# POOL issues both halves of one quad of cache pages, ahead of its operand pads; SP issues neither

## What is computed

```python
def layer(x, p, caches):
    q, kc, ks, kw, gates, u = split(rmsnorm(x, g_attn) @ w_in)       # ONE input projection
    # compressed branch: every block of 32 tokens (stride 16) of K and V goes through a small MLP
    past_cmp = cache_cmp[page_table].reshape(DB, past_len, 2, KVH, DH)  # 8 sequences x 32 pages
    cmp = compress(concat([past_cmp, kc]), w1, w2, pe)
    attn = gates . (attend(q, cmp), attend(q, selected_blocks(ks)), attend(q, window(kw)))
    conv = swish(layernorm(causal_depthwise_conv(u, width=31)))
    x = x + concat([attn, conv]) @ w_out
    x = x + relu(rmsnorm(x, g_mlp) @ w_up)**2 @ w_down
    x = x + (p @ w_ple) * sigmoid(rmsnorm(x, g_ple) @ w_ple_gate)
    return rmsnorm(x, g_final)

def compress(kv, w1, w2, pe):
    c = chunks_of_16_rows(kv)
    pre = c[:-1] @ w1[:, :16] + c[1:] @ w1[:, 16:] + pe_term
    return gelu(pre) @ w2
```

## Time and profile before

| what | value |
|---|---|
| time, median of 3 runs | 1845.31 us (1843.94 to 1849.23) |
| the profiled execution's own time | 1846.45 us |
| its span, first to last instruction | 1844.8 us |
| TensorE clock granted over the span | 0.993 of full |
| DMA | 198.31 MB, mean 107 GB/s |

### The profile page before, as it was taken

How to read it: one execution, slowest core, us unless ns; L and a number is a source line. 1 busy time by engine, 2 the same in 40 slices (tenths; PEclk the granted TensorE clock), 3 DMA queues, 4 the chain that set the end, 5 groups by cost and what they waited for, 6 DMA issues and landing times.

```text
span 1844.8 us, 36000 instructions
## 1 busy us (share of the span) xinstructions
PE 1792.5 (97%) x13796; PEld 1672.8 (91%) x13796; DVE 1058.4 (57%) x1802; ACT 720.5 (39%) x1355; POOL 747.9 (41%) x702
## 2 busy tenths in 40 slices
PE   8999999999999999999998999999989999999998
PEld 7999999999986667676997999999989999999998
DVE  6799965684657677767547844555631212224525
ACT  5312333335336576666424333333421212114435
POOL 2204972233304343444544665656522323225531
PEclk9999999999999999999999999999999999999999
DMA  4321366355313444342414222322531414113114
GB/s 155 129 69 47 112 205 155 97 134 142 107 62 110 144 125 123 116 133 76 140 46 146 97 103 105 116 102 97 188 129 50 137 45 142 41 48 96 58 35 140
DMA packets 178793, 198.31 MB, mean 107 GB/s; under 512 B 22580, under 2 KB 152304, under 8 KB 178103
## 3 DMA queue, kind: packets, MB, share of 16 engines
q1 hardware_dynamic: 168173, 172.67, 30.1%
q0 software_dynamic: 7840, 21.25, 4.1%
q10 hardware_dynamic: 2610, 2.10, 0.4%
HBM read 165.00 MB, written 35.55 MB: 109 GB/s over the span
## 4 chain that ended last, share of the span: by engine, by line
PE 57%; DVE 6%; ACT 2%; issue 2%; POOL 2%; DMA 1%; SPq 0%; ACTq 0%; DVEq 0%; POOLq 0%
PE ps L198 13%; PE ps L2644 11%; PE ps L204 6%; PE ps L2649 6%; PE ps L2416 5%; PE ps L1825 3%; PE ps L1813 3%; PE ps L1837 3%; PE ps L3252 2%; POOL S L1780 2%; PE ps L1864 2%; DVE S L2074 1%; PE ps L3262 1%; PE ps L3278 1%; PE ps L1900 1%
## 5 line engine op out<-in xcount | busy, mean ns | idle before, releaser
L184 POOL TENSOR_TENSOR wd_lo<-wd_raw,wd_hi 128x1024 fp32r<-128x1024 f32 (+1 forms) x40 | 100.5, 2513 | 256.2 <-ACT wd_hi L2961 256.2
L1780 POOL TENSOR_SCALAR S<-S,inv,gate_p 128x640 f32<-128x640 f32 (+7 forms) x186 | 124.9, 689 | 193.2 <-DVE inv L2084 193.2
L3065 DVE TENSOR_TENSOR xT<-ps,xT 128x1056 f32<-128x1056 f32 x40 | 50.3, 1258 | 257.2 <-PE ps L204 257.2
L198 PE MATMUL ps<-Hhi,wd_hi 128*128 128x352 f32 x768 | 167.7, 327 | 5.8 <-ACT wd_hi L2961 5.8
L198 PE MATMUL ps<-Hlo,wd_hi 128*128 128x352 f32 x768 | 166.8, 325 | 0.0
L1164 DVE SCALAR_TENSOR_TENSOR y<-u,conv_w,y 128x1024 f32<-128x1024 f32 x120 | 156.5, 1351 | 1.2
L1008 PE MATMUL ps_p<-Xhi,w1hi 128*128 128x256 f32 x544 | 139.1, 293 | 1.4 <-ACT Xhi L713 1.4
L431 POOL DMA_DIRECT2D raw<-in_cache_cmp_kv_dram x124 | 78.2, 634 | 149.3 <-DVE relaid L1250 120.8
L198 PEld LDWEIGHTS ps<-Hhi,wd_hi 128*128 128x128 f32 x768 | 132.1, 191 | 6.2 <-ACT wd_hi L2961 6.1
L1008 PE MATMUL ps_p<-Xlo,w1hi 128*128 128x256 f32 x544 | 132.7, 283 | 0.0
L198 PEld LDWEIGHTS ps<-Hlo,wd_hi 128*128 128x128 f32 x768 | 132.0, 190 | 0.0
(11 more groups left out here) (475 smaller groups left out, 4502.1 us busy)
## 6 DMA issues: line engine op xcount, KB each, us to landing
s_raw<-in_cache_slc_kv_dram SPq DMA_DIRECT2D x256, 128.0 KB, 2.1
raw<-in_cache_cmp_kv_dram SPq DMA_DIRECT2D x132, 128.0 KB, 4.3
hidden<-cs SPq DMA_DIRECT2D x32, 528.0 KB, 2.6
Hraw<-hidden SPq DMA_DIRECT2D x32, 528.0 KB, 4.9
up_raw<-in_w_up_dram SPq DMA_DIRECT2D x16, 1024.0 KB, 5.4
raw<-in_cache_cmp_kv_dram POOLq DMA_DIRECT2D x124, 128.0 KB, 4.6
win_raw<-in_w_in_dram SPq DMA_DIRECT2D x38, 256.0 KB, 3.4
wd_raw<-in_w_down_dram SPq DMA_DIRECT2D x16, 512.0 KB, 4.1
```

Of the source, the lines that this page charges most:

```text
L184: self.c.nc.gpsimd.tensor_tensor(self.lo[s][:, 0:nk, :], self.raw[s % self.raw_slots][:, 0:nk, :], self.hi[s][:, 0:nk, :].bitcast(F32), AL ...
L198: nc.tensor.matmul(ps[:, j, 0:CH], self.hi[s][:, k, :], x(k)[:, CH * j:CH * j + CH], start=(k == 0 and n == 0), stop=False)
L1780: nc.gpsimd.tensor_scalar(x, x, inv[:, n % 3, 3 * e + br:3 * e + br + 1], c.gate_p[:, i, H * br + h:H * br + h + 1], ALU.mult, ALU.mult).t ...
```

## The change

POOL's loop over its halves of quads gets a second loop behind it, still ahead of the wait for the projection's end: half 0 and half 1 of quad 4, eight transfers. Its later loop begins with quad 5 instead of 4. SP's list loses half 0 of quad 4. The two halves now count their landings on POOL's semaphore of slot 0, and `relay` asks for the counts that follow from that. Nothing else is changed; each engine computes what it did, and the same pages are read.

```diff
--- before.py
+++ after.py
@@ -428,7 +428,7 @@
                 pages = [cs_pages[ds(page, 1)] for page in at]
             for n, page in enumerate(pages):
                 half, i = n % 2, 2 * part + n // 2
-                eng.dma_start(raw[s][DH * half:DH * half + DH, i, :], page.rearrange("o q f -> (o q) f")).then_inc(raw_loaded[0 if g < 2 else part][s], 16)
+                eng.dma_start(raw[s][DH * half:DH * half + DH, i, :], page.rearrange("o q f -> (o q) f")).then_inc(raw_loaded[0 if g < 2 else 1 if g == 4 else part][s], 16)
 
         @block.sync
         def _(sp):
@@ -496,7 +496,7 @@
                     load_quad(sp, mybir.EngineType.SP, part, g)
             store_rows(8)
             spill_q(3)
-            for g in (2, 3, 4):
+            for g in (2, 3):
                 load_quad(sp, mybir.EngineType.SP, 0, g)
             sp.wait_ge(free[0], 10)
             for e in range(3):
@@ -591,11 +591,13 @@
             pool.wait_ge(pages_loaded, 16)
             for g in (2, 3):
                 load_quad(pool, mybir.EngineType.Pool, 1, g)
+            for part in range(2):
+                load_quad(pool, mybir.EngineType.Pool, part, 4)
             pool.wait_ge(W.done, NT)
             for s in range(2):
                 nc.gpsimd.memset(Xhi[s][:, :, 128:NC + 2].bitcast(F32), 0.0).then_inc(padded, 1)
                 nc.gpsimd.memset(Xlo[s][:, :, 128:NC + 2].bitcast(F32), 0.0).then_inc(padded, 1)
-            for g in range(4, 1 + NQD * B):
+            for g in range(5, 1 + NQD * B):
                 load_quad(pool, mybir.EngineType.Pool, 1, g)
 
             f = dict(allow_small_or_imprecise_dtypes=True)
@@ -1236,7 +1238,8 @@
             def relay(g):
                 s = g % 4
                 for part in range(2):
-                    after(dve, raw_loaded[part][s], 64 * (g // 4 + 1) + (64 - 128 * part if s < 2 else 0))
+                    by_pool = (128 * part - 64) if s == 0 and g >= 4 else 0
+                    after(dve, raw_loaded[part][s], 64 * (g // 4 + 1) + (64 - 128 * part if s < 2 else 0) + by_pool)
                 if g == 0:
                     dve.wait_ge(alo_read, 1)
                 elif g == 2:
```

## The result

| what | before | after |
|---|---|---|
| median time, 21 runs each | 1845.82 us (1841.5 to 1849.87) | 1850.84 us (1848.94 to 1856.77) |
| ratio of times | | 1.0025, 95% interval 1.0018 to 1.0032 |
| the profiled execution's own time, and its span | 1846.45, 1844.8 us | 1850.22, 1848.7 us |
| granted clock over the span | 0.993 | 0.99 |

The ratio is + 4.6 us, with an interval of + 3.3 to + 5.9 (the two medians lie 5.0 us apart): the way that was forecast, inside the 0.3% that the prediction called the same, on its slow side. The time lies inside the range (1843 to 1851.5 us), near the upper end, 3.6 us above the 1847.2 us of the forecast itself.

A forecast was written before the change was run, and what follows sets the result against it. PE, busy 97% of the span, was taken to bound the kernel. Pads + 3.94, quad 4's wait - 2.59, its clock - 1.48, clock after the longer hole + 2.0 sum to + 1.87: from 1845.31 to 1847.2 us, range 1843 to 1851.5.

The forecast's parts named there:

- The pads: POOL's memsets behind quad 4's issues: all come 3.94 us later, and PE's first hole grows from 1.40 to 5.34 us.
- rival 3: POOL's quad 4 issues: DVE's copies hold them up, pads 5.0 us later yet, + 6.9 us, 1852.2 us; chance 0.06.
- The wait for quad 4: DVE's relay 4: the data are there over 5 us ahead, so all 2.59 us of PE's second hole go.
- The clock: PE behind its holes: 1.48 us saved with the second hole, 2.0 us (0 to 2.83) lost behind the longer first.
- SP, the later halves, the transfers: SP's lighter list, POOL's halves from quad 5 on, and the same bytes moved: each counted as nothing.
- The sum: Whole kernel: + 3.94 - 2.59 - 1.48 + 2.0 = + 1.87 us, with the clock's ends - 0.13 to + 2.70 us.
- The range: Measured time, held at 0.8: 1843 to 1851.5 us, from the clock's ends, 2 us either way, part of two rivals.
- Rivals 1 and 2: 1: pads cost nothing, the hole goes, 1841.2 us, chance 0.10; 2: quad 4 is still late, 1851.3 us, chance 0.05.
- Rival 4: The change doesn't do what it says; pads slip further only if quad 0's relay is late; held by the rest, 0.03.

The follow-up runs named there:

- half of it: Kernel before, but POOL issues its own half of quad 4 ahead of the pads, SP keeps the other half: 1846.42 us, ratio 0.9997.
- pads by DVE (in either): DVE instead of POOL sets the four pads, in the kernel after (1845.40 us, ratio 0.9990) and in the kernel before (1844.61 us, 0.9989).
- 4 and 11 products: Kernel before with 4 or 11 chained scratch products on POOL ahead of the pads: 1846.48 us, ratio 0.9994, and 1848.40 us, 1.0014.
- pads first: Kernel after, but with the four pads ahead of quad 4's eight issues on POOL: 1847.24 us, ratio 0.9996.
- SP's quads first: Kernel before, but SP issues its halves of quads 2 to 4 ahead of storing the sampled rows: 1844.18 us, ratio 0.9984.
- pages early: Kernel after, with POOL's two readings of quad 4's page numbers put ahead of its wait for quad 2: 1845.06 us, ratio 0.9996.

## Why the prediction was right, and where it was short

One account fits every profile, to within 0.35 us, from the projection's end to the first copy of a compressed K. In the "half of it" run PE works from the first hole to that copy for 15.65 us without a stop at full clock; its own row therefore fits by construction. Add a run's holes, and half of what PE did at the lower clock (PE's busy time in that stretch):

| kernel | first hole | later hole | work at 0.50 | sum | measured |
|---|---|---|---|---|---|
| before, three profiles | 1.40 each | 2.59, 3.79, 2.91 | 3.41, 5.46, 3.41 | 21.35, 23.57, 21.67 | 21.12, 23.24, 21.46 |
| after, three profiles | 6.53, 6.40, 6.61 | none | 4.88, 3.04, 6.03 | 24.62, 23.57, 25.28 | 24.41, 23.41, 24.99 |
| pads by DVE (in either) | 1.58 | 1.66 | none | 18.89 | 19.15, 19.14 |
| half of it | 2.63 | none | none | 18.28 | 18.28 |
| 4 and 11 products | 3.18; 6.52 | none | 3.41; 5.51 | 20.54; 24.93 | 20.37; 24.65 |
| pads first | 1.40 | 2.28 | 3.42 | 21.04 | 20.91 |
| SP's quads first | 1.40 | none | none | 17.05 | 17.06 |
| pages early | 3.39 | none | 3.42 | 20.75 | 20.63 |

*The pads: right in kind, 1.2 us short.* The forecast had the first memset 3.94 us later. From the projection's end it came after 0.06 us before and 5.17, 5.06 and 5.26 after, so 5.1 later. Of the missing 1.2, 0.86 is the idle of 2.24 for 1.38 and 0.30 the idle of 0.36 inside the first half, 0.06 elsewhere. The cause of the 0.30 is not found. The step that failed stands in rival 3: "So at most the first issue meets one". It counted issues and left out the reading of page numbers ahead of the first, which is what ran beside DVE's split and relay 1, and the forecast gave even that one issue no price; its pace of 3.64 us for a half quad was read at 272 us, where relay 4 was still waiting. The Trainium skill (SBUF — State Buffer, two separate sides) has the rule for issues, and the 1.70 us issue agrees; quad 3's four issues in 2.27 us beside relay 0 show no such hold-up, and the slow reading of page numbers stands in our rows alone.

*The wait for quad 4: right, and somewhat larger.* It goes whole, and the landing was early by far: the last of quad 4 was there at 271.85, and its relay began at about 280. Over three profiles of before PE's second hole is 3.1 us, not the 2.59 of one.

*The clock: right by luck of a mean.* Half of the work at 0.50 is on average 2.0 us before (1.7, 2.7, 1.7) and 2.3 after (2.4, 1.5, 3.0). I had - 1.48 and + 2.0; the measured difference of + 0.3 stands where I had + 0.5, and the 3.0 lies beyond the 2.83 that I had as an end. One and the same program lost 1.5 to 3.0 us behind holes of 6.40 to 6.61 us. The Trainium skill's rule that the monitor behind the clock runs free of the kernel's start (TensorE: Matmul & The Clock Gate, Part 1) agrees with these rows, which don't show the monitor itself.

*SP, the later halves, the transfers: nothing, as said.* No new wait for a transfer appears, and the last stretch shows PE as full as before. The lag at the first compressed K (+ 3.51 us: 286.63 for 283.12, where 1 to 3 was forecast) is that at PE's next hole (+ 3.54: 549.72 for 546.18).

*The sum.* With three profiles on each side it is 24.27 - 21.94 = + 2.3 us, of which the holes are + 2.0 and the clock + 0.3; the spans say the same, 1849.5 - 1847.1 = + 2.4. The forecast was + 1.87. The first pair of profiles gave + 3.3, because before's first had the shortest wait. The timed runs say + 4.6, at least + 3.3. What lies between + 2.3 and that is not found in any stretch: behind the first compressed K the three profiles average 1562.9 us before and 1562.4 after. But the profiled executions of before took 1846.45, 1849.35 and 1850.47 us, all above the median of 1845.82; those of after took 1850.22, 1852.35 and 1850.27, about their median of 1850.84. So the + 2.3 is likely too low. Three profiles a side, which differ by 2 us among themselves, can't show more.

*The range: in part luck.* The sum with the clock's upper end and 2 us for the scatter of the medians reaches only 1850.0 us. The measured 1850.84 us is inside because the range also took in a part of rivals 2 and 3.

*Rivals 1 and 2* are out: the pads came late, and nothing waited for quad 4. *Rival 3* came true in a sixth of its price, about 0.9 us of its 5, as far as DVE is the cause, and without the sign that it named: no issue of quad 4 in after took over 0.60 us. *Rival 4* is out, for the lists did what they say.

Why did a stall of 3 us that was really there, and was really removed, leave a loss? Because the pads and quad 4 are two paths side by side to the same PE. Lateness of the pads up to about what quad 4 is late is free (1.8 us cost nothing that the runs can see with 4 products); beyond that PE's hole grows with it one to one (3.18 us with 4 products, 6.52 with 11, where the pads came 1.8 and 5.1 us late). The change brought the later path forward by 3 us and put the earlier one back by 5. SP's list had the free room: there SP's own half could go first without passing anything that PE waits for.

## What to carry to other kernels

Before a transfer is issued earlier, look at what it is moved past on the issuing queue: eight issues and the readings of their page numbers were 8.5 us of that engine here (258.92 to 267.39), and they belong on a queue whose next work nobody waits for. Where two things are late at one place, removing one is worth only their difference, and delaying the other is paid from there on. Take the price of a stall from several profiles of the unchanged kernel, not from one, and see where the time of each lies among the timed runs.

## What the runs showed of the hardware that I had not expected

- At one place, beside the end of DVE's split of 128x1024 and its copies of 128x512, POOL lost 0.9 us in a reading of four page numbers (1.20 for 0.34) and, with the reading moved away, 1.2 us in an issue (1.70 for 0.52). Other readings and issues beside such splits and copies ran at their usual pace (0.33 us, and 2.27 for four issues); what decides it is not shown.
- A hole's length alone does not decide whether the clock falls: behind 2.28 us (pads first) it went to 0.50, behind 2.63 us (half of it) it stayed at 1.00, as it did behind 1.58 and 1.66 us.
- POOL's product of 128x128 operands took 0.47 us by itself (5.16 for 11), a memset of 128x1040 0.93 us on DVE and 0.97 on POOL.
